# Layer 0's experts gathered as 8 KB pairs of rows, laid out as four ranks of 32 tokens in five places

## The chip, the cores and the metric

The program runs on one core of a Trainium2 chip. The metric is device time in microseconds (us), the median of the runs. The core has five engines that the text names as the profile does: PE (matrix products; PEld is its weight load), DVE (vector), ACT (scalar, with a table of functions), POOL (here it only issues the gathers) and SP (here it only issues the plain loads). Sixteen DMA engines move the data between HBM and the on-chip memory of 128 partitions; the products' sums lie in eight banks (PSUM).

## The reference, cut to what matters

All arrays are float32. The first half of the model has two layers. In layer 0 both streams, `x` and `ctx` (256 tokens of 1024 numbers each), end in a product-key expert stage; in layer 1 only `x` does. Then follows a second block of dense layers, which the change doesn't touch.

```python
def _peer(h, w_pq, peer_keys, peer_down, peer_up):
    q = (h @ w_pq).reshape(B, L, PEER_HEADS, 2, PEER_QDIM // 2)
    s = einsum("blhpd,hpkd->blhpk", q, peer_keys)
    sv, si = lax.top_k(s, 16)                      # per head and half
    cand = sv[..., 0, :, None] + sv[..., 1, None, :]
    top_s, pos = lax.top_k(cand, 16)               # 16 experts of 16384
    gate = softmax(top_s)
    def one(hh, ee, gg):                           # ee: 8 heads x 16 ranks a token
        a = einsum("tkd,td->tk", peer_down[ee], hh)
        act = gg * gelu(a)
        return einsum("tk,tkd->td", act, peer_up[ee])
```

So each token needs 128 rows of `peer_down` and the same 128 rows of `peer_up`, 4 KB each. For the two streams of layer 0 that is 2 x 256 x 128 pairs of rows, 512 MiB in all.

## The kernel before

One gather of the program serves 128 tokens (a tile of a stream) and has 128 columns, one for each head and rank. Layer 0 has four of them, `GATHERS` 0 to 3: x0 tile 0, x0 tile 1, c0 tile 0, c0 tile 1 (c0 is the context stream). Layer 1 has two, x1 tile 0 and 1.

**The gather of layer 0.** It goes in 16 groups of 8 columns. For a column POOL issues one indirect DMA from `peer_down` (line 2814, `rows<-in_peer_down,idx`): partition p receives the row of token p, 4 KB. DVE multiplies it with `h_ps` (two banks that hold h of the 128 tokens, copied there by ACT, L1753) and sums, which gives one number a token (L2324, `a8`). After the eighth column DVE and ACT compute gelu and gate for the 8 columns together (DVE L2330 and L2332, the tanh on ACT L1795, DVE L2338 and L2341). The rows of `peer_up` come in another layout: one DMA fetches four ranks for 32 tokens, since PE can then sum four ranks in one product. So the activations must change places: DVE masks them (L2348, `act_masked`), PE moves them with four small products (L1197, `move`), ACT copies the result (L1786) and makes eight 128x32 matrices of them (L1791, `quad_w`), and PE takes two products of 32 x 512 for each of the eight (L1210, `up`) into banks 4 and 5. The indices are moved in the same way once for each set of heads: DVE masks (L2273), PE moves (L1154), ACT copies (`moved`). The marks `route` and `moved` tell POOL that the indices of a set are there, before and after that move.

**Places.** All rows land in `rows`, eight places of 4 KB a partition. POOL fetches `peer_down` of group g into a place when `peer_up` of group g - 2 in it has been used, and `peer_up` of group g - 1 when the `peer_down` row in it has been used.

**Side work.** Beside the groups the engines do other stages: the rest of the routing (`route`, on DVE), its scores (`pq`, 16 + 4 products on PE, L1126 and L1136), and the whole context stream of layer 0 and a part of layer 1 (`gpre`, `att`, `gate`, `out`, `norm`, `hT`, `zF`, `kv` ...). The functions `beside_x0` and `beside_c0` write a list of 32 x 2 half-slots for the two tiles of a stream; every engine works in the order of that list. In one group PE does `move` of the group before, the stages of the first half-slot, the `up` products of the group before and then the stages of the second half-slot. DVE does the 8 downs, the first half-slot, the end of gelu, the second half-slot. SP loads the side work's weights, mostly 1 MB a stage, up to three stages ahead.

**Layer 1's gather** (`gather_both`, `both_ups`) already fetches pairs: `peer1` holds a down row and an up row side by side, one indirect DMA (L2860) brings 8 KB a partition into one of eight places (four in `rows`, three in `kvmem`, one in `h_ctx`), in the layout of 128 tokens by one rank.

## Time and profile before

| | us |
|---|---|
| median of 3 runs | 3811.63 |
| range of the runs | 3804.46 to 3811.77 |
| the profiled execution's own time | 3813.63 |
| its span | 3811.8 |
| first gather of layer 0 issued | 364.9 |
| last gather of layer 0 issued | 1869.6 |
| first and last gather of layer 1 issued | 2023.7, 2695.2 |

The span is divided into a start (to 365 us), the four gathers of layer 0 with their side work (to 1880 us), the attention of layer 1, its two gathers (2024 to 2710 us), and the second block. The profile's part 2 shows these as stretches of the DMA row. "DMA share" is the mean busy share of the sixteen DMA engines, in which overlapping packets can bring it a little over 1. The time between an instruction and the one before it on its engine is called idle, and the name behind the arrow is what ended it.

### The profile page before, as it was taken

Reading aid. Unit: us, or ns where it says so; the run is one execution under the profiler, and the core shown is the slowest. Engines: PE = TensorE matmul, PEld = TensorE weight load, DVE = VectorE, ACT = ScalarE, POOL = GpSimd, SP = SyncE. Lnnn points to the kernel's source line nnn. Section 1 sums busy time; section 2 is a strip of 40 time slices with the busy share of each in tenths; the row PEclk is TensorE's granted clock in tenths of the full one; section 3 lists DMA queues with packets and bytes.
Section 4 is the critical chain, followed back from the end, with each engine's and each line's share of the span. In section 5 each row is a group of like instructions: output and inputs, shape, how many; then the busy total and the mean of one; then the engine's idle time right before and its main releaser. Section 6 shows DMA issues by size and latency. Waiting matters only on the chain.

```text
span 3811.8 us, 42583 instructions
## 1 busy us (share of the span) xinstructions
PE 3054.7 (80%) x15018; PEld 1920.9 (50%) x15018; DVE 2452.1 (64%) x5511; ACT 969.7 (25%) x2143; POOL 1229.4 (32%) x1309
## 2 busy tenths in 40 slices
PE   6899776778775766676788877777798899999899
PEld 2487432333341221232256433323597789897798
DVE  3444888565578786555456887776565866565564
ACT  1432111220111111111131111112233543334433
POOL 0001566565567666666402333333100000000000
PEclk8999987888887887888789999999999999999999
DMA  7665999999999999999728999999654145454354
GB/s 301 260 253 218 385 408 397 388 392 377 396 405 389 410 407 394 410 409 410 303 72 336 389 405 411 413 406 416 241 189 160 61 149 194 162 199 167 127 178 153
DMA packets 237314, 1156.88 MB, mean 304 GB/s; under 512 B 26961, under 2 KB 27729, under 8 KB 165970
## 3 DMA queue, kind: packets, MB, share of 16 engines
q0 software_dynamic: 184320, 805.39, 52.9%
q1 hardware_dynamic: 52818, 349.25, 24.9%
q8 instruction: 98, 1.61, 0.2%
q14 instruction: 78, 0.64, 0.0%
HBM read 1153.49 MB, written 1.05 MB: 303 GB/s over the span
## 4 chain that ended last, share of the span: by engine, by line
PE 43%; DMA 26%; DVE 16%; POOL 7%; issue 5%; ACT 2%; SPq 0%; DVEq 0%; ACTq 0%; POOLq 0%
DMA rows<-in_peer_up,diag 13%; PE ps L1272 9%; PE ps L1273 9%; PE ps L1274 9%; POOL rows L2814 7%; DMA rows<-in_peer_down,idx 5%; DMA h_ctx<-in_peer,idx 4%; PE ps L1210 4%; PE ps L1175 4%; DMA rows<-in_peer,idx 3%; DVE rows L2324 3%; PE ps L883 1%; DVE shared L2557 1%; PE ps L1126 1%; DVE rows L2290 1%
## 5 line engine op out<-in xcount | busy, mean ns | idle before, releaser
L1210 PE MATMUL ps<-rows,diag 128*32 128x512 f32 x2048 | 589.0, 760 | 397.9 <-DMA rows<-in_peer_up,diag 392.8
L2324 DVE CUSTOM_DVE_ANT_0 rows<-rows,ps 128x1024 f32<-128x1024 f32 x512 | 614.4, 1219 | 348.9 <-DMA rows<-in_peer_down,idx 334.7
L2814 POOL DMA_INDIRECT rows<-in_peer_down,idx x512 | 487.9, 953 | 648.6 <-DVE gates L2277 364.4
L2814 POOL DMA_INDIRECT rows<-in_peer_up,diag x512 | 482.4, 942 | 251.1 <-DVE a L2324 140.7
L1210 PEld LDWEIGHTS ps<-rows,diag 128*32 128x32 f32 x2048 | 82.1, 120 | 866.1 <-DMA rows<-in_peer_up,diag 839.0
L1272 PE MATMUL ps<-hT_hi,w_hi 128*128 128x256 f32 x1792 | 508.6, 284 | 8.9 <-DVE hT_lo L2469 8.9
L1273 PE MATMUL ps<-hT_hi,w_lo 128*128 128x256 f32 x1792 | 508.8, 284 | 0.0
L1274 PE MATMUL ps<-hT_lo,w_hi 128*128 128x256 f32 x1792 | 507.8, 283 | 0.0
L2874 POOL TENSOR_TENSOR ss<-nwt,minus_half 128x1 f32<-128x1 f32 x24 | 13.2, 549 | 1097.5 <-DVE nwt L2009 1097.5
L1272 PEld LDWEIGHTS ps<-hT_hi,w_hi 128*128 128x128 f32 x1792 | 343.3, 192 | 14.4 <-issue 14.3
L2459 DVE TENSOR_TENSOR w_lo<-wring,w_hi 128x2048 fp32r<-128x2048 f32 x120 | 274.6, 2291 | 114.8 <-ACT w_hi L1852 113.5
L1274 PEld LDWEIGHTS ps<-hT_lo,w_hi 128*128 128x128 f32 x1792 | 342.9, 191 | 0.0
L1273 PEld LDWEIGHTS ps<-hT_hi,w_lo 128*128 128x128 f32 x1792 | 341.9, 191 | 0.1
L1175 PE MATMUL ps<-rows,diag 128*128 128x512 f32 x512 | 250.1, 640 | 80.3 <-ACT diag L1769 73.3
L1852 ACT ACTIVATE w_hi<-wring 128x2048 fp32r<-128x2048 f32 x120 | 229.3, 1912 | 117.4 <-DMA wring<-in_wdn 85.6
L1175 PE MATMUL ps<-kvmem,diag 128*128 128x512 f32 x384 | 192.5, 649 | 71.0 <-ACT diag L1769 71.0
L2860 POOL DMA_INDIRECT rows<-in_peer,idx x128 | 122.4, 957 | 391.7 <-PE ps L1175 230.5
L1175 PEld LDWEIGHTS ps<-rows,diag 128*128 128x128 f32 x512 | 100.3, 203 | 225.2 <-issue 111.8
L2290 DVE CUSTOM_DVE_ANT_0 rows<-rows,ps 128x1024 f32<-128x1024 f32 x128 | 153.7, 1218 | 67.4 <-DMA rows<-in_peer,idx 63.9
L1126 PE MATMUL ps<-hT,wring 128*128 128x256 f32 x768 | 174.3, 386 | 1.9 <-ACT hT L1531 1.9
L1074 PE MATMUL ps<-hT,wring 128*128 128x256 f32 x768 | 174.4, 386 | 1.6 <-ACT hT L1531 0.9
L1175 PEld LDWEIGHTS ps<-kvmem,diag 128*128 128x128 f32 x384 | 75.3, 206 | 186.3 <-ACT diag L1769 107.1
(342 smaller groups left out, 4847.0 us busy)
## 6 DMA issues: line engine op xcount, KB each, us to landing
wring<-in_wgu SPq DMA_DIRECT2D x66, 1024.0 KB, 4.9
wring<-in_wdn SPq DMA_DIRECT2D x33, 1024.0 KB, 4.9
wring<-in_wG SPq DMA_DIRECT2D x32, 1024.0 KB, 7.9
wring<-in_wmod SPq DMA_DIRECT2D x28, 1024.0 KB, 8.1
wring<-in_wpq SPq DMA_DIRECT2D x24, 1024.0 KB, 8.0
rows<-in_wgu SPq DMA_DIRECT2D x22, 1024.0 KB, 4.9
rows<-in_wmod SPq DMA_DIRECT2D x20, 1024.0 KB, 7.8
rows<-in_wdn SPq DMA_DIRECT2D x11, 1024.0 KB, 4.9
```

The lines of the kernel that those rows point to most:

```text
L1074: last = pe.matmul(b[:, dt * TOK:(dt + 1) * TOK], w[:, k * 256 + dt * P:k * 256 + (dt + 1) * P], hT[:, k, :], start=(k == 0), stop=(k == K ...
L1126: last = pe.matmul(b[:, hp * TOK:(hp + 1) * TOK], w[:, k * 256 + hp * P:k * 256 + (hp + 1) * P], hT[:, k, :], start=(k == 0), stop=(k == K ...
L1175: ins = pe.matmul(ps[:, UPB + half, :], diag[:, s, :], both[s][:, D + half * 512:D + (half + 1) * 512], start=(first and j == 0), stop=(la ...
L1210: ins = pe.matmul(ps[qd:qd + QUAD, UPB + half, :], quad_w[:, j, :], rows[:, j, half * 512:(half + 1) * 512], start=(first and j < QUADS), ...
L1272: pe.matmul(out_, lh[l_at], rh[r_at], start=start, stop=False, skip_group_check=skip)
L1273: pe.matmul(out_, ll[l_at], rh[r_at], start=False, stop=False, skip_group_check=skip)
L1274: return pe.matmul(out_, lh[l_at], rl[r_at], start=False, stop=stop, skip_group_check=skip)
L1852: act.activation(W2_HI[c % SLOTS2], W2[c % SLOTS2], ACT.Copy).then_inc(hi_ready, 1)
L2290: dve.tensor_tensor_reduce(out=both[c][:, 0:D], in0=both[c][:, 0:D], in1=h_ps, scale=1.0, scalar=0.0, op0=ALU.mult, op1=ALU.add, accum_out ...
L2324: dve.tensor_tensor_reduce(out=rows[:, j, :], in0=rows[:, j, :], in1=h_ps, scale=1.0, scalar=0.0, op0=ALU.mult, op1=ALU.add, accum_out=a8[ ...
L2459: dve.tensor_tensor(W2_LO[c % SLOTS2], w, W2_HI[c % SLOTS2].bitcast(f32), ALU.subtract).then_inc(lo_ready, 1)
L2814: pool.indirect_dma_start(out=rows[:, j, :], out_offset=None, in_=table, in_offset=bass.IndirectOffsetOnAxis(ap=of[:, g * GROUP + j:g * GR ...
```

## The change

- Layer 0 gets a joined table `peer0` as layer 1 has one: a down row and its up row side by side. There are 128 gathers of 8 KB a partition for each tile in place of 128 of 4 KB from each table: 512 indirect DMAs in place of 1024, the same bytes.
- Both halves come in the layout of four ranks by 32 tokens. `SPREADS` lists the 512 gathers: in each set of heads a quarter of the tokens (j) after the other. Partition 32 i + m then holds token 32 j + m, so `h_ps` must hold h of one quarter four times: `spread_h` on PE writes it with eight products of a 32-column piece of the identity. It runs once for each quarter and set, 16 times in a tile 0 and 8 times in a tile 1, 48 times in all, and waits until the downs of the old quarter are done; the next down on DVE waits for it (`h_spread`).
- `move`, `act_masked`, the ACT copy and the four DVE operations of gelu on 8 columns are gone. ACT does gelu for each gather alone, six operations in a row (`spread_diag`), of which five work on 128x1 and the last writes the 128x32 matrix. The gates are moved with the indices, once for each set (`gates_moved`).
- PE's up products follow one by one: `between()` stands ahead of the side work's products and issues the next up once four of them have been counted, for three of the four gathers of a half-slot. The rest of the three follows the half-slot's stages, then `spread_h` where a quarter begins, then the fourth up. DVE and ACT do four gathers and then the stages of a half-slot.
- There are five places of 8 KB: four in `rows`, and `x[1]` (the context stream's tile) up to gather 164, from then on a part of `kvmem`. SP loads `ctx` again (1 MB) ahead of the stage `out` of c0. POOL issues a gather when the up of the one five before it is done, and it waits for `moved` where it waited for `route`.
- Bank 3, which `move` used, joins the banks of the side work (four in place of three). `kT` is laid out in two halves so that one is free earlier, and c0's gates lie in `h[1]` in place of `h[0]`. The stage `moved` of the first set is in `scoring`, behind `pq` 2.

```diff
+SPREAD_PLACES = 5
+LENT = 164
+def spread_gathers(t):
+    return [(TOP * h0 + QUADS * s + j, j, n) for n, (h0, h1) in enumerate(SETS[t]) for j in range(QUADS) for s in range(TOP * (h1 - h0) // QUADS)]
...
-    return [[("take", r)], [("pq", r, 0)], [("pq", r, 1)], routes(r, 0, (0, 8))[0:4], [("pq", r, 2)]]
+    return [[("take", r)], [("pq", r, 0)], [("pq", r, 1)], first[0:4], [("pq", r, 2)], first[4:]]
...
-        ROT_GATHER = [0, 1, 2]
-        MOVE = 3
+        ROT_GATHER = [0, 1, 2, 3]
...
+            def between():
+                pieces[0] += 1
+                if pieces[0] >= 4 and next_up[0] < last_up[0]:
+                    ups_to(next_up[0] + 1)
...
+                        between()
                         last = pe.matmul(b[:, dt * TOK:(dt + 1) * TOK], w[:, k * 256 + dt * P:k * 256 + (dt + 1) * P], hT[:, k, :],
...
+            def spread_h(n):
+                pe.wait_ge(mark["h"], h_mark(run, 1, 2))
+                if n == 0:
+                    taken(pe, run, TAKEN)
+                else:
+                    pe.wait_ge(down_done, n)
+                one_of = ident[:, QUAD * j:QUAD * (j + 1)]
+                for half in range(2):
+                    for i in range(QUADS):
+                        qd = QUAD * i
+                        ins = pe.matmul(h_ps[qd:qd + QUAD, half * 512:(half + 1) * 512], one_of, h[RUNS[run][0]][:, t, half * 512:(half + 1) * 512],
+                                        start=True, stop=True, tile_position=(0, qd), skip_group_check=True)
+                ins.then_inc(h_spread, 1)
+            def spread_up(n):
+                if n % P == 0:
+                    pe.wait_ge(sum_read, n // P)
+                pe.wait_ge(diag_ready, n + 1)
+                for half in range(2):
+                    ins = pe.matmul(ps[qd:qd + QUAD, UPB + half, :], quad_w[:, n % GROUP, :], spread_place(n)[:, D + half * 512:D + (half + 1) * 512],
...
+                    last_up[0] = n + HALF - 1
+                    run_stages(stages)
+                    ups_to(n + HALF - 1)
+                    last_up[0] = 0
+                    if n + HALF < len(SPREADS) and new_quarter(n + HALF):
+                        spread_h(n + HALF)
+                    ups_to(n + HALF)
...
+            def spread_diag(n):
+                act.wait_ge(down_done, n + 1)
+                act.activation(sq, a, ACT.Square, scale=GELU_A ** 0.5).then_inc(gelu_step, 1)
+                act.activation(weight, a, ACT.Copy, scale=gates_moved[t][:, col:col + 1]).then_inc(gelu_step, 1)
+                act.activation(inner, sq, ACT.Identity, scale=a, bias=a).then_inc(gelu_step, 1)
+                act.activation(th, inner, ACT.Tanh, scale=GELU_C).then_inc(gelu_step, 1)
+                act.activation(act_, th, ACT.Identity, scale=weight, bias=weight).then_inc(gelu_step, 1)
+                act.activation(quad_w[:, c, :], quad_id, ACT.Copy, scale=act_).then_inc(diag_ready, 1)
...
+            def spread_down(n):
+                if new_quarter(n):
+                    dve.wait_ge(h_spread, len([m for m in range(n + 1) if new_quarter(m)]))
+                dve.wait_ge(row_in[k], 16 * (n // SPREAD_PLACES + 1))
...
+                if n >= SPREAD_PLACES:
+                    pool.wait_ge(upp_done, n - SPREAD_PLACES + 1)
+                pool.indirect_dma_start(out=spread_place(n), out_offset=None, in_=A["peer0"],
...
-        "peer_down": i["peer_down"][0], "peer_up": i["peer_up"][0],
+        "peer0": np.concatenate([i["peer_down"][0], i["peer_up"][0]], 1), "peer1": np.concatenate([i["peer_down"][1], i["peer_up"][1]], 1),
```

PE at the start of x0 tile 0, before (after `pq` 3; L1126 and L1136 are the products of `pq`, L1154 moves indices, L1197 and L1210 are `move` and `up`):

```order
L1126 MATMUL ps<-hT,wring 128x256 x16
L1136 MATMUL ps<-keysT,shared 128x128 x4
L1197 MATMUL ps<-act_masked,quad 32x8 x4
L1154 MATMUL ps<-shared,quad 32x16 x4
L1126 MATMUL ps<-hT,wring 128x256 x16
L1136 MATMUL ps<-keysT,shared 128x128 x4
L1210 MATMUL ps<-rows,diag 32x512 x16
```

The same place in the changed kernel (L1149 and L1160 are `pq`, L1217 is `spread_h`, L1230 is `spread_up`, two products for one gather):

```order
L1217 MATMUL ps<-h_in,ident 32x512 x8
L1230 MATMUL ps<-rows,diag 32x512 x2
L1149 MATMUL ps<-hT,wring 128x256 x3
L1230 MATMUL ps<-x_ctx,diag 32x512 x2
L1149 MATMUL ps<-hT,wring 128x256 x4
L1230 MATMUL ps<-rows,diag 32x512 x2
L1149 MATMUL ps<-hT,wring 128x256 x4
L1230 MATMUL ps<-rows,diag 32x512 x2
L1149 MATMUL ps<-hT,wring 128x256 x5
L1160 MATMUL ps<-keysT,shared 128x128 x4
L1217 MATMUL ps<-h_in,ident 32x512 x8
```

One block of 16 products for eight columns has become two products at a time, each of which waits for its own gather, between 3 to 5 products of `pq`; and eight products that spread h stand ahead of the last up of the half-slot.

ACT in the half-slot of x0 tile 0 with `moved` and the first `gpre` (L1701, L1721), before:

```order
L1786 ACTIVATE act_moved<-ps 128x8
L1791 ACTIVATE diag<-quad,act_moved 128x32 x8
L1531 ACTIVATE diag<-ps 128x32
L1701 ACTIVATE h_in<-ps,hbg 128x256 x2
L1795 ACTIVATE th<-g 128x8
```

and in the changed kernel, where the first six rows stand four times ahead of the half-slot's stages:

```order
L1796 ACTIVATE g<-a 128x1
L1797 ACTIVATE gated<-a,diag 128x1
L1799 ACTIVATE g<-g,a 128x1
L1801 ACTIVATE th<-g 128x1
L1803 ACTIVATE act<-th,gated 128x1
L1805 ACTIVATE diag<-quad,act 128x32
L1756 ACTIVATE diag<-ps 128x32
L1551 ACTIVATE diag<-ps 128x32
L1721 ACTIVATE h_ctx<-ps,hbg 128x256 x2
```

The ten operations for eight columns have become 24 for four gathers, and the side work's copies stand behind the fourth of them.

POOL at the start, before and then in the changed kernel (L2814 and L2813 issue the gathers):

```order
L2814 DMA rows<-in_peer_down,idx 128x1024 x16
L2814 DMA rows<-in_peer_up,diag 128x1024 x8
L2814 DMA rows<-in_peer_down,idx 128x1024 x8
L2814 DMA rows<-in_peer_up,diag 128x1024 x8
L2814 DMA rows<-in_peer_down,idx 128x1024 x8
```

```order
L2813 DMA rows<-in_peer,diag 128x2048 x4
L2813 DMA x_ctx<-in_peer,diag 128x2048
L2813 DMA rows<-in_peer,diag 128x2048 x4
L2813 DMA x_ctx<-in_peer,diag 128x2048
L2813 DMA rows<-in_peer,diag 128x2048 x4
```

The blocks of down and up rows by turns have become one kind of gather of twice the width, which takes the five places in turn.

## Rows read from the trace of the kernel before

**Rows 1.** The page: the span, and the DMA in 40 slices of it
```profile
span 3811.8 us, 42583 instructions
...
DMA  7665999999999999999728999999654145454354
GB/s 301 260 253 218 385 408 397 388 392 377 396 405 389 410 407 394 410 409 410 303 72 336 389 405 411 413 406 416 241 189 160 61 149 194 162 199 167 127 178 153
```

**Rows 2.** Busy us by stretch; last: granted clock, DMA share, GB/s
```profile
core 0: us, PE busy (x) PEld busy (x) DVE busy (x) ACT busy (x) POOL busy (x), PEclk, DMA share, GB/s
364.00:1886.00 1522.00, 1083.08 (x4723) 458.95 (x4721) 1024.17 (x2564) 239.44 (x892) 970.29 (x1024) 0.84 1.00 396
1600.00:1850.00 250.00, 172.58 (x737) 67.81 (x736) 136.88 (x277) 35.79 (x141) 169.10 (x180) 0.83 1.03 410
2050.00:2700.00 650.00, 505.70 (x1133) 216.96 (x1131) 506.80 (x1471) 125.65 (x401) 236.44 (x247) 0.94 0.99 406
```

**Rows 3.** DMA view, 364 to 1886 us: packets, MB, share of 16 engines
```profile
DMA packets 157757, 602.91 MB, mean 396 GB/s; under 512 B 17520, under 2 KB 17776, under 8 KB 151280
q0 software_dynamic: 147456, 536.94, 89.4%
q1 hardware_dynamic: 10224, 65.02, 10.5%
```

**Rows 4.** Columns of rows 2, in stretches of 80 and 10 us
```profile
364.00:444.00 80.00, 63.95 (x329) 44.44 (x328) 59.96 (x176) 12.69 (x39) 45.20 (x47) 0.91 0.93 364
394.00:404.00 10.00, 6.31 (x23) 5.08 (x24) 9.59 (x25) 2.27 (x11) 2.93 (x4) 0.51 0.62 221
690.00:700.00 10.00, 10.00 (x48) 3.62 (x47) 3.10 (x17) 2.33 (x9) 2.81 (x3) 1.00 0.77 293
2090.00:2100.00 10.00, 10.00 (x45) 7.74 (x44) 8.87 (x33) 0.90 (x3) 2.26 (x3) 1.00 1.00 423
```

**Rows 5.** Groups, 365 to 1888 us: count, busy us, mean ns, idle before
```profile
L2324 DVE CUSTOM_DVE_ANT_0 rows<-rows,ps 128x1024 f32<-128x1024 f32 x512 | 614.4, 1219 | 348.9 <-DMA rows<-in_peer_down,idx 334.7 <-ACT ps L1753 0.5
L1210 PE MATMUL ps<-rows,diag 128*32 128x512 f32 x2048 | 589.0, 760 | 397.9 <-DMA rows<-in_peer_up,diag 392.8 <-DVE mb L2369 3.0 <-ACT diag L1791 1.1
L2814 POOL DMA_INDIRECT rows<-in_peer_down,idx x512 | 487.9, 953 | 648.6 <-DVE gates L2277 364.4 <-PE ps L1210 185.7 <-issue 93.8
L1791 ACT ACTIVATE diag<-quad,act_moved 128x32 f32<-128x32 f32 x512 | 115.4, 307 | 2.1
L2348 DVE TENSOR_TENSOR act_masked<-act,quad 128x32 f32<-128x32 f32 x64 | 12.3, 193 | 2.2
L1786 ACT ACTIVATE act_moved<-ps 128x8 f32<-128x8 f32 x64 | 11.4, 178 | 372.3 <-PE ps L1197 372.1
```

**Rows 6.** Tile in_peer, the 8 KB gather of layer 1
```profile
L2860 POOL DMA_INDIRECT rows<-in_peer,idx x128: 932/936/1767, 2023.7 to 2685.4; - x128
DMA to landing us min/median/max: 5.4/12.1/22.6
```

**Rows 7.** Timeline: start us, us, engine, line, out<-in, [idle before]
```profile
326.43 1.90 PE L828 MATMUL ps<-wring,cvec 128*2 128x512 f32 x16
340.04 3.01 PE L828 MATMUL ps<-rows,cvec 128*2 128x512 f32 x16
364.86 1.12 POOL L2814 DMA_INDIRECT rows<-in_peer_down,idx  x1 [364.41 <-DVE gates L2277]
366.55 7.07 PE L1126 MATMUL ps<-hT,wring 128*128 128x256 f32 x32
373.46 1.05 PE L1136 MATMUL ps<-keysT,shared 128*128 128x128 f32 x8
...
443.50 1.22 DVE L2324 CUSTOM_DVE_ANT_0 rows<-rows,ps 128x1024 f32<-128x1024 f32 x1
453.90 0.28 DVE L2224 MAX8 shared<-shared 128x8 f32<-128x128 f32 x1
460.53 0.17 DVE L2338 SCALAR_TENSOR_TENSOR g<-th,a 128x8 f32<-128x8 f32 x1
```

More of the change, by code:

```diff
@@ L417 @@
 ORDER = with_parts(order())
[L419 removed]
+STAGES = [st for e in ORDER for st in (e[4] + e[5] if e[0] == "gather" else [e])]
 def parted_chunks():
@@ L1229, in gather @@
-                if beside_a or beside_b:
-                    group(n0, beside_a)
-                else:
-                    groups(pe, n0, n1, group)
-                run_stages(beside_b)
-                if n1 == GROUPS and G + 1 not in JOINED:
-                    move(GROUPS - 1)
-                    up(GROUPS - 1, last=True)
+                        if i == 2 * PAIRS - 2:
+                            both_ups(i + 1)
+                        continue
+                    n = P * G + HALF * (2 * n0 + part_)
@@ L2279, in route @@
                 at_mark(dve, "route", run, no)
+                if run != "x1":
+                    masked(gates[t], 512).then_inc(mark["sent"], 1)
             def both_downs(t, n):
```

337 lines of the change are left out of this document (126 added, 211 removed).

## Prediction

> **What bounds the kernel now.** I read the DMA rows of the page first. From 381 us on, fifteen slices in a row stand at 9, at some 400 GB/s [rows 1]: that is the gathers of layer 0. In the windows, the stretch of 1522 us from the first gather to the last has a DMA share of 1.00, while PE is busy for 1083 us, DVE for 1024, POOL for 970 and ACT for 239 [rows 2]. So the sixteen DMA engines set the time there, and no engine does over the whole. They moved 602.91 MB, of which 536.94 are gathers and 65.02 side weights [rows 3]. For the last stretch with light side work the rate stands at 410 GB/s at a share of 1.03 [rows 2]: I take 410 for the ceiling with 4 KB rows. At it the 602.9 MB need 1470 us, so 52 us of the 1522 are not the ceiling's. They are short dips in which places don't come free: 221 GB/s at 394 us, with DVE busy for 9.59 of 10 us, or 293 at 690 us, with PE busy for 10.00 [rows 4]. About 8 us of the 52 are the first 80 us (364 GB/s [rows 4]: 29.1 MB, 71 us at 410), about 7 the last gathers, which drain, and 37 the dips.
>
> What lies before 365 us and after 1880 us stays as it is, but for where it starts: layer 1's attention waits for the end of layer 0's gathers. A us won or lost in this stretch is one of the total.
>
> **What 8 KB rows give.** The nearest row is layer 1's gather, in which each DMA already brings 8 KB a partition. It has 10 us windows at 423 GB/s [rows 4], at a share of 1.00, where 4 KB rows need 1.03 for 410. So the ceiling is some 3% higher. The gathers: 536.9 MB take 1309.6 us at 410 and 1269.3 at 423. Side weights stay, and the 1 MB of `ctx` that is loaded again adds 2.6 us. Sum: 1270 + 161 + 2.6 = 1433 in place of 1470, or **-37 us**. The bounds: 0 (if the rate belongs to layer 1's layout, 128 tokens by one rank), and -47 if side weights run at 423 too.
>
> The Trainium skill's page "DMA: Bandwidth & Descriptors", section "Anatomy of one DMA — SWDGE (gpsimd) path", gives each DMA about 2.0 us fixed beside its bytes at 436 GB/s. If these weren't hidden, 512 fewer DMAs would be worth an estimated 1024 us. The trace speaks against it: 410 GB/s with 4 KB rows [rows 2] is only 3% below the best with 8 KB [rows 4], so the fixed part lies beside other transfers.
>
> **POOL.** 512 issues at 0.95 us go [rows 5], 488 us of its 970. It was not the limit: 0.
>
> **DVE.** 512 downs of 1.22 us stay [rows 5]. Gelu on eight columns goes, five small operations for each of 64 groups; the largest of them costs 12.3 us in all [rows 5], so some 56 us together. The masked gates come back 12 times, at 0.2 to 0.4 us. Net -50 us on an engine at 67%. That is slack, not time: 0.
>
> **ACT.** Six operations for each gather. Small ones take 178 ns (a copy of 128x8), the matrix of 128x32 307 ns [rows 5], so a chain is 5 x 0.2 + 0.3 = 1.3 us, and 512 of them 666 us; 115 + 11 us and 64 small ones go. ACT comes to some 770 us of 1500, still half idle. On the path of one gather it is 1.3 us between down and up.
>
> **PE.** The up products are the same two for each MB: 589 us for 512 [rows 5], 1.15 each. `spread_h` is new. Its nearest row is `mod`'s products, eight of 512 columns side by side in four column groups: 1.90 us, and 3.01 in another case [rows 7]. I take 2.5; 48 of them are 120 us (91 to 144), and `move` gives an estimated 20 back (four products of 8 columns for each of 64 groups). PE goes from 1083 to some 1180 us of 1500. Over the whole it has room; at the head it hasn't.
>
> **The head.** The first gather now waits for `moved`, which stands behind `pq` 2 on PE. The first was issued at 364.9 us; PE ended `pq` 2 at 366.6 [rows 7], and the move and two copies follow: 368 us, **+3 us**. Then the first up (gather 0: 5.4 us to land [rows 6], 1.3 down, 1.3 ACT) isn't possible before 376 us, and PE, which used to run ahead with `pq` 3, stands at it. A half-slot with a `pq` costs PE 7.07 + 1.05 [rows 7] + four ups of 1.05 + 2.5 for the spread = 14.8 us, where four gathers and a weight chunk cost the DMA 5.2 MB / 423 = 12.4. The first has two `pq`: 22.9 us from 376 to 399; three more bring PE to 443.5 with 16 gathers done and at most 5 more landed, 21 MB. Before, at 443.5, DVE began group 3 [rows 7]: 24 downs and 16 ups done, 20 MB, and up to 4 more landed. The deficit is up to 3 MB, or 7 us, and the next half-slots of set 0 and 1 have a spread each. I take **+10 us** for both (bounds +3 and +20).
>
> **The places.** Here it can fail. A place is held from landing to the next issue: down 1.3, ACT 1.3, up 1.05, issue 0.3: 4.0 us. A gather needs at least 5.4 to land [rows 6]: a cycle of 9.4 us. The pace is 602.9/512 = 1.18 MB a gather, 2.8 us at 423, so five places give 14.0 us: 4.6 to spare. Two route stages keep DVE for 453.90 to 460.53 = 6.6 us [rows 7]; a gather that lands 2.8 us after the last down waits 5.1 for DVE, then up to 1.8 for PE's pieces. So such half-slots starve the DMA by 2 to 3 us for one gather; those with lighter work don't. Before had eight places of 4 KB with dips of 37 us in all. I take a third more, **+12 us** (bounds: -20, if finer grains remove half of the dips, and +80). Two waits inside a half-slot (`moved` 9 of c0 in the slot of its route, `kv` 1) hold three ups each: **+2**.
>
> Sum: -37 + 10 + 12 + 2 = **-13 us**. The profiled execution (3813.6, span 3811.8) would come to 3801; on the median 3811.6 it is 3799.
>
> **Rivals.**
> - *Slower: held places.* One mechanism: the up of the fourth gather stands behind the half-slot's side products and the spread, and the next down behind DVE's stages, so that on average more than 5 - 5.4/2.8 = 3 places are held. It decides where the mean hold exceeds 3 x 2.8 = 8.4 us. A gpre half-slot (7.1 us of products) with 4 us of DVE work gives by the same steps 6.5 to 7.1 us, one with both routes 8.7. If the some 58 half-slots with routing (26 beside x0 tile 0, 32 beside c0 tile 0 or the end of x0) lose 1.2 us each, that is 70 in place of 12: 3857. For it: DVE at 67% over the stretch and higher there; layer 1's gather, with eight places of 8 KB, still only makes 406 on the mean [rows 2]. Against: half of the stretch has light side work. Milder forms lie between, from +8 on.
> - *No gain in rate.* 4 KB or 8 KB, the new layout keeps 410: -13 + 37 = +24, 3836. Against it: the packets are as in layer 1.
> - *A draw.* Dips of 20 us more than I took use the gain up: 3804 to 3819.
> - *The dips go.* Ups one by one free the places earlier than blocks of eight: -37 + 5 - 18 = -50, 3762. For it: the ceiling was held all through the light stretch.
> - The change does what it says by its code; I give a mistake in it no weight.
>
> **Numbers.** My forecast (3799, own range 3780 to 3804) and its like with fewer dips: 0.48 for faster by over 0.2%, or 7.6 us, about what a measurement can tell here; of these 0.12 for the last rival. The draw 0.20. Slower 0.32: held places 0.24, no gain 0.08. The range leaves out 0.1 on either side: 3762 to 3850.
>
> **What would show it.** In the new profile: windows of the light stretch (the last 300 us of layer 0) at 421 to 424 GB/s, else the first term is wrong. 16 gathers done by 445 us, else the head. In the windows between 450 and 1500 us more stretches under 350 GB/s than before, POOL's idle time ended by PE's up (L1230) and not by issue: held places. DVE's idle before the down ended by PE's spread: its price. PE busy near 1180 us and ACT near 770 in the stretch. The prediction is wrong if the last gather of layer 0 isn't issued between 1820 and 1910 us.

## The result, and the profile after

On the chip of the first comparison the changed kernel takes **3940.97 us** (median of 4 runs, 3938.67 to 3946.9), the kernel before 3810.27 (median of 4, 3804.46 to 3811.77): a ratio of **1.0348, 95% interval 1.033 to 1.0366**. It is 131 us slower, where I had forecast 13 us less. The page of the changed kernel, its span and the DMA in 40 slices, against [rows 1]:

```profile
span 3937.5 us, 44302 instructions
...
DMA  7766999899999888899952999999945325454444
GB/s 302 272 235 240 331 391 363 345 376 387 390 375 366 349 338 340 347 393 365 394 200 106 390 392 416 399 421 409 376 168 184 117 84 196 166 198 171 150 162 159
```

Slices 5 to 19 lie in the gathers of layer 0. They stood at 377 to 410 GB/s before, and stand at 331 to 393 now. The windows (busy us of each engine with its count; last granted clock, DMA share, GB/s) show the whole stretch, the light end, the head and the stretch of layer 1, and then four windows of 10 us:

```profile
core 0: us, PE busy (x) PEld busy (x) DVE busy (x) ACT busy (x) POOL busy (x), PEclk, DMA share, GB/s
364.00:2010.00 1646.00, 1237.32 (x5006) 478.24 (x4998) 964.96 (x2231) 874.99 (x3307) 487.86 (x512) 0.87 0.93 366
1600.00:1850.00 250.00, 182.87 (x650) 56.92 (x649) 115.14 (x213) 144.44 (x538) 78.12 (x84) 0.84 0.95 379
364.00:444.00 80.00, 69.14 (x363) 40.87 (x356) 36.10 (x102) 31.04 (x112) 19.00 (x20) 0.94 0.90 331
2235.00:2835.00 600.00, 467.43 (x1011) 195.71 (x1010) 466.44 (x1340) 116.44 (x372) 221.58 (x231) 0.93 0.99 407
...
390.00:400.00 10.00, 9.95 (x57) 6.72 (x55) 2.23 (x3) 2.10 (x7) 0.93 (x1) 1.00 0.56 209
1460.00:1470.00 10.00, 6.89 (x34) 3.89 (x34) 9.62 (x28) 5.41 (x23) 0.94 (x1) 0.61 0.18 75
1570.00:1580.00 10.00, 0.04 (x1) 0.07 (x1) 5.39 (x21) 6.58 (x28) 0.00 (x0) 0.50 0.00 0
1700.00:1710.00 10.00, 9.44 (x36) 4.04 (x32) 4.92 (x8) 6.30 (x25) 3.72 (x4) 0.83 0.99 392
```

Against [rows 2]: the stretch grew from 1522 to some 1646 us, its DMA share fell from 1.00 to 0.93, its rate from 396 to 366 GB/s. No engine is full instead: PE is busy for 1237 of 1646 us, DVE for 965, ACT for 875. Layer 1, which the change doesn't touch, runs at 407 GB/s (406 before [rows 2]) and starts later. So the DMA, which bounded this stretch, now waits, and for places. The waits, 365 to 2010 us (us in total, times, longest):

```profile
POOL rows L2813 <- PE ps L1230: 902.8, 382, 14.1
PEld ps L1230 <- ACT diag L1805: 614.5, 308, 8.6
ACT g L1796 <- DVE a L2337: 571.5, 290, 11.0
DVE rows L2337 <- DMA rows<-in_peer,diag: 382.7, 218, 10.2
...
POOL kvmem L2813 <- PE ps L1230: 157.3, 63, 20.0
```

It is a ring: POOL waits for PE's up product (474 times over all places), PE for ACT's matrix, ACT for DVE's product, DVE for a gather to land. A ring in which everybody waits and nobody is full is bound by its length.

**Where the 131 us are.** I cut the stretch into windows of 10 us (370 to 1870 before, 370 to 2010 after) and counted in each what it lost against 422 GB/s, 10 x (1 - rate/422):

| | windows under 350 GB/s | 350 to 390 | 390 and more | sum |
|---|---|---|---|---|
| before | 14, lost 36 us | 7, 9 us | 129, 37 us | 82 us |
| after | 50, lost 154 us | 41, 48 us | 73, 15 us | 217 us |

The first two columns are the loss, 118 and 39 us. In the third one the loss fell from 37 to 15 us, but most of that is only that there are fewer such windows: 129 that lose 0.29 us each before, 73 that lose 0.21 us each now. The rate in them rose from 410 to 413 GB/s, which over 73 windows is worth 6 us. That is all that arrived of the gain that I had forecast. The sum is +135 us; the spans of the two profiled executions differ by 126, the medians by 131.

### The profile page after: what moved, and what is told of

Its sections match the earlier page's. It is cut to its first block, busy times and chain, and to the rows that moved or that the text cites. A ratio compares the mean times of both kernels' runs of the same rounds, so it can differ in the third digit from the quotient of the medians.

```text
span 3937.5 us, 44302 instructions
## 1 busy us (share of the span) xinstructions
PE 3214.3 (82%) x15370; PEld 1946.6 (49%) x15370; DVE 2399.4 (61%) x5191; ACT 1613.1 (41%) x4579; POOL 747.3 (19%) x797
## 3 DMA queue, kind: packets, MB, share of 16 engines
HBM read 1154.53 MB, written 1.05 MB: 293 GB/s over the span
## 4 chain that ended last, share of the span: by engine, by line
PE 52%; DMA 21%; DVE 17%; ACT 6%; issue 3%; POOL 0%; SPq 0%; DVEq 0%; POOLq 0%; ACTq 0%
DMA rows<-in_peer,diag 10%; PE ps L1292 9%; PE ps L1294 9%; PE ps L1293 8%; PE ps L1230 6%; PE ps L1200 4%; DMA h_ctx<-in_peer,idx 3%; DMA rows<-in_peer,idx 3%; PE ps L1095 3%; PE ps L1149 3%; DVE rows L2337 2%; PE ps L1121 2%; PE ps L893 2%; DMA kvmem<-in_peer,diag 2%; DVE shared L2547 1%
## 5 line engine op out<-in xcount | busy, mean ns | idle before, releaser
L2337 DVE CUSTOM_DVE_ANT_0 rows<-rows,ps 128x1024 f32<-128x1024 f32 x410 | 493.9, 1220 | 477.5 <-DMA rows<-in_peer,diag 384.5
L1230 PE MATMUL ps<-rows,diag 128*32 128x512 f32 x1640 | 515.4, 720 | 289.4 <-ACT diag L1805 283.3
L2813 POOL DMA_INDIRECT rows<-in_peer,diag x410 | 390.9, 953 | 1295.0 <-PE ps L1230 902.8
L1230 PEld LDWEIGHTS ps<-rows,diag 128*32 128x32 f32 x1640 | 71.6, 118 | 611.5 <-ACT diag L1805 515.7
L1796 ACT ACTIVATE g<-a 128x1 f32<-128x1 f32 x512 | 101.0, 197 | 573.8 <-DVE a L2337 572.8
L1200 PE MATMUL ps<-rows,diag 128*128 128x512 f32 x512 | 259.9, 660 | 83.4 <-ACT diag L1789 76.3
L1783 ACT ACTIVATE th<-g 128x2 f32<-128x2 f32 x128 | 26.0, 203 | 494.0 <-DVE g L2316 494.0
L1803 ACT ACTIVATE act<-th,gated 128x1 f32<-128x1 f32 x512 | 198.1, 387 | 17.1
L1095 PE MATMUL ps<-hT,wring 128*128 128x256 f32 x768 | 204.3, 412 | 0.0
L1095 PEld LDWEIGHTS ps<-hT,wring 128*128 128x128 f32 x768 | 146.2, 201 | 98.8 <-issue 80.4
```

The lines of the kernel that those rows point to most:

```text
L1095: last = pe.matmul(b[:, dt * TOK:(dt + 1) * TOK], w[:, k * 256 + dt * P:k * 256 + (dt + 1) * P], hT[:, k, :], start=(k == 0), stop=(k == K ...
L1200: ins = pe.matmul(ps[:, UPB + half, :], diag[:, s, :], both[s][:, D + half * 512:D + (half + 1) * 512], start=(first and j == 0), stop=(la ...
L1230: ins = pe.matmul(ps[qd:qd + QUAD, UPB + half, :], quad_w[:, n % GROUP, :], spread_place(n)[:, D + half * 512:D + (half + 1) * 512], start ...
L1803: act.activation(act_, th, ACT.Identity, scale=weight, bias=weight).then_inc(gelu_step, 1)
L2337: dve.tensor_tensor_reduce(out=down, in0=down, in1=h_ps, scale=1.0, scalar=0.0, op0=ALU.mult, op1=ALU.add, accum_out=a8[:, c:c + 1]).then_ ...
L2813: pool.indirect_dma_start(out=spread_place(n), out_offset=None, in_=A["peer0"], in_offset=bass.IndirectOffsetOnAxis(ap=idx_moved[t][:, col ...
```

## Experiments

The runs were made in four groups, each on another chip: e1 to e4; c1, m1, e5 and e6; e7 to e9 and v1; m2 and c2. On all four the kernel before takes 3892 to 3905 us and not 3810. So the changed kernel was run there too, in the second group (c1: 1.0139 times the kernel before). Every other kernel is compared with c1 by way of the two ratios to the kernel before; for the first and the third group this takes for granted that 1.0139 holds on their chips, which wasn't measured. By the intervals of the two ratios such a difference is known to within 12 to 18 us. m1, m2 and c2 are single runs.

### The changed kernel again, and the kernel before

> The changed kernel itself, unedited, on the chip of this group, so that the others of the group have it beside them: 1.035 times the kernel before, if that ratio doesn't depend on the chip. On the chip of the first four experiments the kernel before took 3903 us against 3810; if its transfers alone were slower there, a kernel bound by latency and holds would lose less on such a chip, and the ratio would be under 1.035 (1.00 to 1.02) where the kernel before takes about 3900.

3950.59 us; ratio 1.0139 (1.0112 to 1.0165). The changed kernel is nearly where it was (3941 on the first chip); it is the kernel before that is slower here (3898).

> The kernel before, unedited, for its trace on this chip, where it takes about 3900 us against 3810 on the chip of the first comparison, while the changed kernel takes 3951 against 3941. Theory A (the kernel before is bound by the engines of the DMA in its light stretches, the changed one by its holds): the windows of its layer 0 that showed 410 GB/s show 395 to 400 here, its layer 1 (407 GB/s) the same lower rate, and no wait of another kind grows. Rival: the rate in light stretches is 410 here too (the depth test showed 410 for rows of 4 KB on such a chip) and the time has gone into a few stretches.

Columns as above, the kernel before on the chip of this group and then on the first:

```profile
1100.00:1300.00 200.00, 102.17 (x484) 36.98 (x484) 151.35 (x417) 29.04 (x106) 121.66 (x129) 0.74 0.94 355
...
1600.00:1850.00 250.00, 160.96 (x668) 63.08 (x666) 134.76 (x281) 36.91 (x139) 162.65 (x173) 0.83 1.00 393
```
```profile
1100.00:1300.00 200.00, 116.32 (x524) 36.62 (x516) 169.21 (x462) 30.24 (x115) 139.73 (x146) 0.81 1.01 398
```

The light window fell from 410 [rows 2] to 393, a little under the 395 to 400 expected. But from 1100 to 1500 us the rate fell by a tenth, 398 and 401 to 355 and 358, at a share of 0.94 to 0.95, with PE busy for half of the time and POOL for six tenths. And layer 1 is no slower: its 600 us run at 408 GB/s in the kernel before here (2180 to 2780 us) and in c1, against 406 and 407 on the first chip. So it is no lower ceiling, and theory A is out. The waits of POOL for PE's up grew from 189 to 259 us and the longest from 7.1 to 17.3; why PE comes late isn't seen. What slows the kernel before here stays open. It is why the change costs 3.5% on one chip and 1.4% on another. The experiments below change the changed kernel, which takes nearly the same time on both.

### What a number in flight gives

> A kernel of its own: nothing of the reference is computed; x is copied to the output, and gathers of 128 random rows run in phases, each with a fixed number K of them in flight (the next is issued when the one K before it has landed). First six phases of 48 gathers with rows of 8 KB, K = 1, 2, 3, 4, 5, 8; then five of 96 gathers with rows of 4 KB, K = 2, 4, 6, 8, 10. Theory A: with rows of 8 KB the rate rises with K well beyond 2: about 190 GB/s at 1 (5.4 us for 1 MB), 330 to 370 at 2, 390 to 400 at 3, and 420 to 425 only from 4 or 5 on. The step of my sum that it tests took 2 in flight for enough (5.4 / 2.8 us), which would be 420 GB/s at 2. Theory C: at equal bytes in flight (8 and 10 of 4 KB against 4 and 5 of 8 KB) rows of 4 KB give 3% less, 410; if the size of the row is no matter they give the same within 1%.

Columns: POOL's busy us, granted clock, DMA share, GB/s. Rows of 8 KB with 1, 2, 3, 4, 5 in flight, then rows of 4 KB with 4, 6 and 10:

```profile
50.00:250.00 200.00, 32.77 (x35) 1.00 0.52 186
300.00:400.00 100.00, 32.77 (x35) 1.00 0.98 370
430.00:530.00 100.00, 35.67 (x39) 1.00 1.00 400
560.00:650.00 90.00, 33.99 (x37) 1.00 1.01 422
680.00:775.00 95.00, 35.59 (x38) 1.00 1.01 422
...
1200.00:1300.00 100.00, 61.65 (x66) 1.00 0.95 343
1340.00:1440.00 100.00, 73.14 (x79) 1.00 1.03 410
...
1600.00:1690.00 90.00, 67.72 (x74) 1.00 1.03 410
```

And the time from issue to landing with 2, 3 and 4 gathers of 8 KB rows in flight:

```profile
DMA to landing us min/median/max: 5.1/5.4/5.6
...
DMA to landing us min/median/max: 7.1/7.3/9.3
...
DMA to landing us min/median/max: 9.6/9.7/9.8
```

These are the rows that my sum lacked. One gather of 1 MB at a time takes 5.6 us from issue to issue (1.05 MB at 186 GB/s), and two in flight give 370 GB/s, not 422. **Three in flight aren't quite enough for the full rate (400), four are**, and then each of them takes 9.7 us to land (4 x 1.05 MB / 422 would be 9.9). The minimum of 5.4 us [rows 6] is the landing time with one or two in flight, far from the full rate. And theory C holds for the ceiling: rows of 4 KB end at 410, rows of 8 KB at 422. POOL was never seen to issue faster than every 1.24 us, here and in e5 below (start, us, [idle before]):

```profile
1708.52 0.94 POOL L2831 DMA_INDIRECT kvmem<-in_peer_down,diag  x1 [0.30 <-issue]
1709.76 0.93 POOL L2831 DMA_INDIRECT rows<-in_peer_up,diag  x1 [0.30 <-issue]
```

For 0.52 MB that is 422 GB/s: with rows of 4 KB, POOL is within 3% of the bound itself. It isn't what ends at 410, though: with 10 in flight it issued every 1.24 us without waiting for a landing, more than the 410 that were moved.

### The hold alone, without side work

> A kernel of its own: nothing of the reference is computed; x is copied to the output. Gathers of 128 random rows of 8 KB, each held by the same operations as in layer 0 (the DVE product with the hidden vector, ACT's six operations, the up product on PE), with no side work, no other transfers and a fixed number of places: phases of 48 gathers with 4, 5, 6, 7 and 8 places, then five places with the shortened chain, then five with the chain's last operation alone. The depth test gave 2.83 us a gather at 2 in flight, 2.63 at 3, 2.49 at 4 and more. Theory A: places in flight = places - hold / period, so with a hold of about 4.0 us (nothing to wait for but its own operations) 4 places keep 2.5 in flight (2.7 us, 385 GB/s), 5 keep 3.4 (2.57 us, 408 GB/s), 6 and more keep over 4 (2.49 us, 422 GB/s); shortened chain at five 2.55, chain left out 2.50. If the light stretches of layer 0 (387 to 392 GB/s) have their rate from the hold alone, five places give 385 to 395 here too; if they give 405 to 420, the rest of the loss there is from side work.

Four places, five, six, then five with the shortened chain and five with its last operation alone (columns as for the kernels):

```profile
30.00:130.00 100.00, 58.48 (x134) 5.98 (x132) 41.80 (x68) 52.95 (x202) 31.85 (x34) 0.70 0.93 355
170.00:270.00 100.00, 67.06 (x158) 6.92 (x156) 47.67 (x79) 61.58 (x234) 36.53 (x39) 0.62 1.00 408
300.00:390.00 90.00, 62.57 (x146) 6.29 (x144) 44.60 (x73) 57.93 (x220) 33.78 (x37) 0.61 1.01 427
...
685.00:780.00 95.00, 63.92 (x156) 6.61 (x152) 46.28 (x75) 55.75 (x228) 35.59 (x38) 0.66 1.01 422
815.00:910.00 95.00, 64.60 (x156) 6.62 (x152) 46.84 (x77) 12.21 (x38) 35.58 (x38) 0.64 1.01 425
```

Five places just miss the ceiling (408 as expected: 392 in the first 40 us, 414 to 424 from there on), six reach it (427, even 1% above m1's 422), and four fall to 355 (expected 385). The hold was longer than the 4.0 us of my expectation. Read gather by gather from the trace, from landing to the next issue into the place, it is 5.2 to 5.5 us on the mean in these three phases: most ups run here while the clock is at its lower level and take 1.92 us (granted clock 0.61 to 0.70). With the shortened chain, which takes 1.53 us where the full one takes 1.68, five places give 422. There a gather lands after 7.6 us and is held for 4.9, and one is issued every 2.48 us, so that 7.6 / 2.48 = 3.1 in flight are enough. Whether the 0.15 us alone brought this isn't shown by two phases of one run. So with nothing beside it the layout would lose 1 to 3%. The light stretches of layer 0 run at 379 to 392: the rest of their loss is side work that makes the holds longer. One gather of the changed kernel shows its parts (start, us, engine, line, out<-in, [idle before]):

```profile
1701.01 1.22 DVE L2337 CUSTOM_DVE_ANT_0 rows<-rows,ps 128x1024 f32<-128x1024 f32 x1 [1.27 <-DMA rows<-in_peer,diag]
...
1702.27 0.20 ACT L1796 ACTIVATE g<-a 128x1 f32<-128x1 f32 x1 [0.82 <-DVE a L2337]
...
1703.62 0.32 ACT L1805 ACTIVATE diag<-quad,act 128x32 f32<-128x32 f32 x1
...
1704.85 1.05 PE L1230 MATMUL ps<-rows,diag 128*32 128x512 f32 x4
...
1706.18 0.94 POOL L2813 DMA_INDIRECT rows<-in_peer,diag  x1 [1.54 <-PE ps L1230]
```

Down 1.22 us, chain 1.67 (1702.27 to 1703.94), then 0.91 until PE comes from its side products, up 1.05, issue 0.28: **5.2 us** held. In the chain alone a gather that waits for nothing is held for 4.3 us, or 5.2 where the up runs at the lower clock.

But this gather is a short one. All of them in the changed kernel (365 to 2010 us; from issue to landing), and my means from the same trace:

```profile
DMA to landing us min/median/max: 5.3/8.3/17.5
```

| | one issued every | cycle of a place (5 x that) | issue to landing | hold |
|---|---|---|---|---|
| 365 to 2010 us | 3.21 us | 16.1 us | 8.4 us | **7.7 us** |
| 1600 to 1850 us (light) | 2.99 us | 15.0 us | 8.6 us | 6.5 us |

The 7.7 us are 1.6 until DVE takes the gather, 1.2 for the down, 3.2 from there to PE's start (1.7 of them ACT's chain), 1.3 for the up and 0.3 to the next issue.

### Fewer places, more places

> Four places in place of five (the lent one is not used). Theory A (cycle = hold + landing, rate = places / cycle): at 1700 us five places cycle in 12.4 us, 2.48 us a gather; with four, landing would have to fall from 8.1 to 5.6 us to hold that rate, near the least seen (5.3), so about 2.6 to 2.8 us a gather: 60 to 150 us slower, 4000 to 4090 us. Theory B alone (a few stretches in which PE is stuck, and the light stretches bound by the DMA): each of some dozen stretches loses 2.5 us more, 3960 to 3980 us.

```
-SPREAD_PLACES = 5
+SPREAD_PLACES = 4
```

4130.79 us, ratio 1.0575 (1.0542 to 1.0607): by the two ratios 4.3% or **+170 us** against the changed kernel. The light window 1600 to 1850 us is at 310 GB/s. More than the +60 to +150 expected.

> Seven places of 8 KB in place of five for gathers 184 to 349 (two further parts of the keys' and values' room, which is free there); all else as in the changed kernel. Theory A: for those 166 gathers, about 930 to 1490 us in the changed kernel at 358-388 GB/s, cycle stays and seven places give up to the limit of the DMA engines, 410-420 GB/s; 166 x 2.85 us = 473 us become 166 x 2.55 us = 423 us, so 40 to 60 us less than the changed kernel. Theory B: the dips last as long but are partly covered by the two places more (5 us each): 15 to 30 us less. If the DMA engines were the bound there already: 0 to 5 us.

```
+MORE = range(184, 350)
...
+        k = min(range(7 if n in MORE else 5), key=lambda k: last.get(k, k - 7))
...
-            k = n % SPREAD_PLACES
-            return both[k] if k < HALF else lent[n > LENT]
+            k = PLACES[n][0]
+            return both[k] if k < HALF else lent[n > LENT] if k == HALF else both[k]
```

3895.7 us, ratio 0.9993 (0.9974 to 1.0012): **-57 us**, within the 40 to 60 of theory A. The windows of the changed kernel (c1, on the same chip), and of this one:

```profile
930.00:1100.00 170.00, 143.34 (x539) 59.52 (x537) 88.41 (x151) 87.81 (x329) 48.32 (x51) 0.95 0.98 391
1100.00:1300.00 200.00, 150.53 (x704) 61.80 (x702) 138.14 (x370) 106.55 (x398) 58.65 (x62) 0.86 0.92 357
```
```profile
930.00:1100.00 170.00, 148.91 (x561) 63.61 (x562) 91.65 (x156) 89.20 (x339) 51.94 (x55) 0.94 1.01 412
1100.00:1300.00 200.00, 155.71 (x758) 64.30 (x761) 149.26 (x407) 115.40 (x440) 64.40 (x68) 0.91 0.97 394
1600.00:1850.00 250.00, 183.17 (x648) 59.05 (x645) 114.13 (x212) 138.76 (x521) 75.87 (x81) 0.84 0.94 374
```

Where there are seven places the light part gains 21 GB/s, to 412, and the heavy part 37; behind them, at five again, it is 374 as before (379). Nothing but places was added.

### A shorter chain

> Five of the six ACT operations between a gather's down product and its quad matrix are left out (gelu and gate: quad_w is the unit columns times a), so the output isn't the reference's; places, gathers and PE's order stay. Theory A (a place is held too long, so that too few gathers are in flight: about 4.35 us of hold in the light stretch at 1700 us, 1.67 us of it the chain on ACT): the hold falls by about 1.3 us, the gathers in flight rise from 3.2 to 3.7, the windows 1600 to 2000 us rise from 366-401 to 400-415 GB/s, and the kernel takes 3860 to 3900 us against 3941. Theory B (the loss is in stretches where PE runs stages that wait, with gathers stuck behind them): the 10 us windows below 280 GB/s stay as many (about a dozen), and the kernel takes 3915 to 3935. Theory C (rows of 8 KB move no faster than rows of 4 KB, whatever is in flight): windows stay below 410 GB/s, as in the kernel before.

```
-                act.activation(sq, a, ACT.Square, scale=GELU_A ** 0.5).then_inc(gelu_step, 1)
...
-                act.activation(quad_w[:, c, :], quad_id, ACT.Copy, scale=act_).then_inc(diag_ready, 1)
+                act.activation(quad_w[:, c, :], quad_id, ACT.Copy, scale=a).then_inc(diag_ready, 1)
```

3890.91 us, ratio 0.9973 (0.9957 to 0.9989): **-65 us**, in theory A's 3860 to 3900. By the same count of windows against 422 it loses 121 us in windows under 350 and 44 above, where c1 loses 148 and 73. So a shorter hold helps both. One detail missed: I expected 400 to 415 GB/s from 1600 us on, and 1600 to 1850 shows 387; 900 to 1100 went from 392 to 407. A likely reading is that late in the layer side work on PE holds the places, not ACT; it wasn't tested.

### PE's order

> One edit on PE: before each stage of the names moved, hT and kv, PE first issues the ups that the slot still owes; all else stays. Theory B (PE in order, waiting in a stage for DVE or ACT while finished gathers can't be released): the stretch without transfers at 1568 to 1580 us and those at 1460 and 710 us close in part; 35 to 60 us come back, so 3880 to 3906 us. Theory A (few gathers in flight everywhere): the light stretches stay at 366-401 GB/s, and the gain is 5 to 25 us (3916 to 3936), since ups that are forced early wait on ACT's chain themselves. A rival: PE waits in forced ups for gathers that have not landed, the side work comes later, and DVE's next stage with it: 3941 or more.

```
+                    for st in stages:
+                        if st[0] in ("moved", "hT", "kv"):
+                            ups_to(last_up[0])
+                        run_stages([st])
-                    run_stages(stages)
```

3962.95 us, ratio 1.014 (1.0106 to 1.0174): no difference from 1.0139. It does what it says: 1568 to 1580 us, nearly without transfers in the changed kernel, has 346 GB/s. But the light window 1600 to 1850 us falls from 379 to 358, and the sum is nothing: what the forced ups give, the side work that is put back seems to take elsewhere. So this order wins nothing, and the +2 of "three ups each" was not a term to be won. What the stuck stretches cost by themselves the edit can't tell, since it moves the side work too.

> PE looks for an up product after every second side product instead of every fourth; all else stays. Theory A: the hold of a place has a part that is PE's way to the next look (four products of 0.12 to 0.25 us, half of it on the mean); it shrinks by about 0.3 us, 0.06 us a gather, so 10 to 30 us less than the changed kernel. Rival: PE now reaches an up before its matrix is ready and waits there in order, so the side work comes later: the same time within 10 us, or up to 20 us more.

```
-                if pieces[0] >= 4 and next_up[0] < last_up[0]:
+                if pieces[0] >= 2 and next_up[0] < last_up[0]:
```

3964.08 us, ratio 1.0147 (1.0116 to 1.0178): nothing, as the rival said.

> The interleaving on PE is taken out: the ups of a slot come only after its side work (a slot has four gathers; side work of a heavy slot is 8 to 20 us of PE). Theory A: in heavy slots all places are held for the whole of the side work, so holds of 4.35 us become 10 and more there; 150 to 300 us more than the changed kernel, that is 4100 to 4250 on this chip. If the ups were bound by ACT's chain and not by PE, the interleaving would be worth little: under 50 us.

```
-                if pieces[0] >= 4 and next_up[0] < last_up[0]:
+                if pieces[0] >= 400 and next_up[0] < last_up[0]:
```

4006.35 us, ratio 1.0258 (1.023 to 1.0286): +46 us, where theory A had 150 to 300. The interleaving is worth 1.2%. I had overrated it; its other reading (under 50 us if the ups wait for ACT's chain and not for PE) is the one that came, and in the changed kernel PE waits for ACT's matrix 308 times (`PEld` above).

### The spread of h

> The hidden vector is spread to the quads' layout once for each tile of tokens; the other 44 of 48 spreads (eight products each, on PE) and DVE's waits for them are left out, so most sums are of the wrong tokens. My sum had 48 x 2.5 us = 120 us of PE work for them, nearly free, and the changed kernel shows DVE waiting 66 us for them (16 long waits). Theory D (those waits hold all five places at once): 40 to 60 us less than the changed kernel (3950 us beside this chip's 3898). Theory A (only the cycle of a place counts, and PE's time between is not short): 10 to 25 us less.

```
-    return n % P == 0 or SPREADS[n][1:] != SPREADS[n - 1][1:]
+    return n % P == 0
```

3930.39 us, ratio 1.0077 (1.0051 to 1.0103): **-24 us**, in theory A's range (10 to 25). DVE's 72 us of waits for L1217 (65.5 on `rows`, 6.6 on `kvmem`) all but go (1.4 and 3.9), and as much comes back in its waits for the gather itself: on `rows` 379.6 us in c1, 455.4 here. A wait in the ring is not a cost of its own size.

### Halves of a place

> Each place is filled by two gathers of 4 KB rows (down row and up row from the two tables) in place of one of 8 KB rows; order, places, ACT and PE stay as in the changed kernel. Theory A (what counts is bytes in flight and the time a place is held, not the size of a row): the same time within 0.5%, 3925 to 3960 us, windows 1600 to 2000 us again at 366-401 GB/s; POOL's busy time doubles to about 1100 us and costs nothing. Theory C (rows of 8 KB are dearer or cheaper by themselves): with 4 KB rows the same windows would go to the 410 GB/s of the kernel before (then 3870 to 3900 us), or fall by the 3% that I had put on the row size (then 3970 to 4010 us).

```
-                pool.indirect_dma_start(out=spread_place(n), out_offset=None, in_=A["peer0"],
+                for m, table in enumerate(("peer_down", "peer_up")):
+                    pool.indirect_dma_start(out=spread_place(n)[:, m * D:(m + 1) * D], out_offset=None, in_=A[table],
```

4050.82 us, ratio 1.0385 (1.0347 to 1.0423): **+96 us**. Theory A had the same time: wrong. I had left out that the second half is asked for 1.24 us later, which should make each place's cycle longer by that. A cycle 1.24 us longer over five places is up to 0.25 us a gather, 127 us; the 3% of the row size would be 30 to 40. The two aren't separated here.

> The same ten times 4 KB of places, but filled by down rows and up rows apart: four half places for down rows, six for up rows, and the up row of a gather is asked for three gathers later than its down row, so that ACT's chain runs while the up row is under way and a place is held for the DVE product (about 1.3 us) or the PE product (about 1.05 us) alone, not for both and the chain (4.35 us). PE, DVE and ACT do the same work. Theory A (place time): nearly all of the ten halves are in flight, the light stretches reach the 405-410 GB/s that the kernel before had with rows of 4 KB, and the kernel takes 3790 to 3850 us on a chip on which the kernel before takes 3810 and the changed one 3941. Theory B (PE stuck in stages): the dips stay, since the up rows still wait for PE; 3900 to 3940. Rival D (POOL: two issues of 0.95 us for each gather): POOL is busy 1.9 of 2.5 us and its waits line up, 3900 or more.

```
+LAG = 3
...
+                    pool.wait_ge({"down": down_done, "up": upp_done}[kind], prev + 1)
...
+                fetch_half("down", n)
+                if n >= LAG:
+                    fetch_half("up", n - LAG)
```

4230.29 us, ratio 1.0847 (1.0824 to 1.087): **+276 us**, when I expected the best time of all. The waits of the whole stretch:

```profile
POOL rows L2831 <- DVE a L2362: 588.1, 84, 20.6
...
DVE rows L2362 <- PE ps L1236: 358.5, 39, 20.2
```

By the code a half place is held for one product only, but whether the holds shrank wasn't measured, and POOL issues both kinds in one order. When DVE stands, four down places are used up within some 10 us (4 x 2.5), and POOL then waits for DVE up to 20.6 us, while it can't issue an up row either. DVE stands longer too, up to 20.2 us for a spread, for which PE comes only after its own waits for up rows. And POOL, at 2.5 us a pair, has no room to catch up. The share of the three wasn't measured, so the cause of the 276 us stays open between them.

### A version with two edits

> A version with two edits: seven places for gathers 184 to 349 (55 us less than the changed kernel when alone), and one dependent ACT operation less in each chain: tanh takes 0.0447 a^2 with scale and bias 0.798 a in one operation, in place of a multiply-add and a tanh (the chain 1.67 to about 1.35 us; the same result). Leaving the chain out altogether (1.35 us less hold) gave 60 us, so 0.3 us gives 10 to 20 us: 3875 to 3890 us against 3898 of the kernel before on this chip. If ACT's total time and not the chain counted, nothing: 3895.

```
-                act.activation(inner, sq, ACT.Identity, scale=a, bias=a).then_inc(gelu_step, 1)
-                act.activation(th, inner, ACT.Tanh, scale=GELU_C).then_inc(gelu_step, 1)
...
+                act.activation(inner, a, ACT.Copy, scale=GELU_C).then_inc(gelu_step, 1)
+                act.activation(th, sq, ACT.Tanh, scale=inner, bias=inner).then_inc(gelu_step, 1)
```

With the seven places of e6: 3882.97 us, ratio **0.994 (0.992 to 0.9959)**. It beats the kernel before of its group by 0.6% and the changed kernel by 2.0%. Against e6 it is 21 us faster, within 11 us, as expected; but the chain became shorter by 0.14 us only (1.67 to 1.53), not by 0.3. At e1's price, 65 us for 1.35 us, that would be worth 7 us, and whether the rest is the difference between the chips isn't known. On the first chip it wasn't run; where the kernel before takes 3810 us it would likely not win.

## Why the prediction was wrong

**What bounds the kernel: right**, and the reason for the loss: the DMA was the bound of the stretch, and so whatever keeps it from being full is paid in whole.

**Places: the step that failed.** I wrote that a cycle is 4.0 us of hold + 5.4 of landing = 9.4, against 14.0 that five places give: "4.6 to spare". The cycle that was run is 16.1 us: **7.7 of hold + 8.4 of landing**. Both terms were too small, by 3.7 and by 3.0 us. The landing of 5.4 is the *minimum* of [rows 6]; the median there is 12.1, with eight places, and by m1 and m2 a gather takes 7.6 to 9.7 us to land at the full rate. The hold of 4.0 is the sum of the operations with no wait between them. The chain itself is 0.4 longer (1.67 and not 1.3); the rest is waiting, 1.6 us for DVE and 1.5 between the down, ACT and PE, which I had charged to a few half-slots only. With 8.4 us of landing, 14.0 - 8.4 = 5.6 us of hold are what five places allow at the full rate, and even the light stretch has 6.5. A gather every 3.21 us instead of every 2.8 is some 210 us for 512, and the table above counts 217. The rival "held places" had the mechanism and the same wrong landing (5.4/2.8 = 2 in flight). So it asked for a mean hold over 8.4 us, and the loss came at 7.7; it stood at 3857, 84 us too low. Its signs are all there: 50 windows under 350 GB/s instead of 14, POOL ended by L1230 (1122 us, 474 times), last gather issued at 2004 us and not before 1910. e4 and e6 change the number of places in both directions and e1 the hold, and each time the time moves as this says; m2 has the ring without side work.

**Dips +12: failed as its consequence**: +118 us in windows under 350 GB/s. One of them, with PE's and DVE's rows:

```profile
1558.99 1.22 DVE L2275 TENSOR_TENSOR shared<-shared,iota 128x1024 f32<-128x1024 f32 x1
...
1568.46 0.65 PE L1179 MATMUL ps<-shared,quad 128*32 128x64 f32 x16 [6.87 <-DVE shared L2287]
...
1579.96 0.66 PE L929 MATMUL ps<-ident,shared 128*128 128x128 f32 x2 [10.85 <-DVE shared L2138]
...
1582.76 0.94 POOL L2813 DMA_INDIRECT kvmem<-in_peer,diag  x1 [19.96 <-PE ps L1230]
```

A route stage keeps DVE from 1558 to 1568 us; PE waits in `moved`, and then 10.85 us in the next stage for DVE's norm, and no gather is issued for 20 us. Before, such a window had slack: the windows with DVE busy for 8 us or more of 10 (66 of them) had 393 GB/s on the mean; now (29 of them) 329.

**Rate -37: half right.** The ceiling of 8 KB rows is 422 where 4 KB has 410 (m1). But it is only a ceiling. The light stretch should have shown 421 to 424 and shows 379. Of the 37 us, 6 arrived (the third column of the table). The bound of -47 was added up wrongly: with side weights at 423 too it is -43.

**Head +10: right, a little high.** First gather at 365.5 us (I said 368); POOL's 14.1 us wait from 384 to 398.7 is the half-slot with two `pq` that I had from 376 to 399; the 21st issue at 444.0 us means 16 ups done, as forecast for 443.5 to 445. In MB: 80 us at 331 instead of 364 GB/s [rows 4] is 2.6 MB, 6 us.

**Spread: right in size, not quite free.** 66.1 us beside c0 and 54.7 beside x0 are 121 in all for 48 spreads, against 120. It was to cost nothing; leaving out 44 of them wins 24 us, within 15 (e7). PE as a whole is busy for 1237 us and not 1180: its ups take 634 us where I had kept 589.

**ACT +1.3 us a gather: too low, and no longer slack.** The rows of the changed kernel, 365 to 2010 us (count, busy us, mean ns):

```profile
L1803 ACT ACTIVATE act<-th,gated 128x1 f32<-128x1 f32 x510 | 197.4, 387 | 17.1
L1799 ACT ACTIVATE g<-g,a 128x1 f32<-128x1 f32 x510 | 190.4, 373 | 0.0
L1797 ACT ACTIVATE gated<-a,diag 128x1 f32<-128x1 f32 x510 | 142.5, 280 | 0.0
L1801 ACT ACTIVATE th<-g 128x1 f32<-128x1 f32 x510 | 103.5, 203 | 16.2
```

I took 200 ns for a small one. That is right without an operand of 128x1 as scale or bias; with one it is 280, with two 373 to 387. ACT's total came to 875 and not 770. The Trainium skill's page "ScalarE: Activation LUTs", section "What ACT_TABLE_LOAD costs", says that each such operand adds about 93 ns: by these rows that holds.

**POOL 0, DVE 0: right** for this kernel as to their busy time (488 and 965 us). **Waits in a slot +2:** not what decides (e2).

**Chances.** 0.24 for held places was too little. I had weighed "half of the stretch has light side work" against it; the light half lost too.

## What to carry to other kernels

The landing time that belongs in a cycle is not the least in the trace but the one at full rate, and the hold that belongs in it is the mean with its waits, not the sum of the operations. Where a change trades many small buffers for few large ones, first ask how many must be under way, and take the time a place may be held from what is left. Work that moves between a buffer's landing and its release (here the gelu, which used to run while the up rows were under way) is paid by every buffer, even when its engine is half idle. And a change that gives 3% on the ceiling is worth nothing where the ceiling isn't reached.

## What the runs showed of the hardware

- How steeply the rate depends on the number in flight: 186, 370, 400, 422 GB/s with 1 to 4 gathers of 1 MB, which land after 5.4, 5.4, 7.3 and 9.7 us (m1), and that a row of half the size costs 3% of the ceiling but reaches it with 3 MB in flight, where 3 MB in rows of 8 KB give 400.
- POOL issues an indirect DMA every 1.24 us at best in these runs (m1, e5): 0.94 busy and 0.30 between.
- ACT operations of 128x1 take 197 to 203 ns, 280 with one operand of 128x1 as scale or bias and 373 to 387 with two. The chain of six, with the 128x32 at its end, takes 1.67 us.
- The same kernel before takes 3810 us on one chip and 3892 to 3905 on four others, while the changed kernel takes 3941 on the first and 3951 on one of the four; from 1100 to 1500 us the transfers of the former run at 355 to 358 GB/s (c2) instead of 398 to 401. This wasn't explained.
